# Two of the four weight sums of each seven-product group: made by adding transfers on GpSimd's queue in place of VectorE and GpSimd additions

## What is computed

```
first block :  x = x + relu(h @ ffn_w1)^2 @ ffn_w2           (8192 rows of ffn_w2)
second block:  x = x + norm((silu(gate) * val) @ ffn_w_down)  (5632 rows of ffn_w_down)
```

## Time and profile before

| | us |
|---|---|
| median of three runs | 2196.92 |
| the profiled execution's own time | 2197.45 |
| its span, first instruction to last | 2195.6 |
| TensorE busy in the span | 2180.6 |
| VectorE busy | 1566.8 |
| ScalarE busy | 1133.7 |
| GpSimd busy | 710.6 |

### The profile page before, as it was taken

The page is one execution under the profiler, slowest core; times in us unless marked ns, Lnnn a source line. Parts: engine busy times, 40 slices in busy tenths (PEclk is TensorE's granted clock), DMA queues, the critical chain, the costliest instruction groups (busy, mean ns, idle before and its releaser), DMA issues.

```text
span 2195.6 us, 34076 instructions
## 1 busy us (share of the span) xinstructions
PE 2180.6 (99%) x11511; PEld 1863.4 (85%) x11511; DVE 1566.8 (71%) x2187; ACT 1133.7 (52%) x1720; POOL 710.6 (32%) x625
## 2 busy tenths in 40 slices
PE   9999999999999999999999999999999999999998
PEld 8888988888888888888887887788888888888887
DVE  6877766558658757755868667568778777787775
ACT  6445555555445445444555455465555455554553
POOL 3202320361362263153000033005554355533531
PEclk9999999999999999999999999999999999999999
DMA  7665335556556556565555654545555655555554
GB/s 253 233 224 172 109 135 187 167 188 211 191 182 210 187 187 205 206 195 194 181 192 178 229 168 141 192 163 181 189 195 184 201 198 193 187 191 197 200 207 148
DMA packets 118084, 414.35 MB, mean 189 GB/s; under 512 B 12896, under 2 KB 18048, under 8 KB 117472
## 3 DMA queue, kind: packets, MB, share of 16 engines
q1 hardware_dynamic: 111600, 401.37, 54.4%
q10 hardware_dynamic: 6384, 11.70, 1.7%
HBM read 409.29 MB, written 2.15 MB: 187 GB/s over the span
## 4 chain that ended last, share of the span: by engine, by line
PE 91%; DVE 4%; POOL 2%; issue 2%; ACT 1%; DMA 0%; POOLq 0%; DVEq 0%; ACTq 0%
PE bank L607 31%; PE bank L615 16%; PE bank L941 6%; PE bank L943 6%; PE bank L942 6%; PE bank L664 3%; PE bank L666 3%; PE bank L665 3%; DVE wboth L1307 1%; POOL bias L2661 1%; PE bank L720 1%; PE bank L1269 1%; PE bank L1267 1%; PE bank L1268 1%; PE bank L721 1%
## 5 line engine op out<-in xcount | busy, mean ns | idle before, releaser
L1307 DVE TENSOR_TENSOR wboth<-raw,wboth 128x1024 fp32r<-128x1024 f32 (+1 forms) x756 | 954.2, 1267 | 470.5 <-ACT wboth L2157 462.2
L2157 ACT CAST wboth<-raw 128x1024 fp32r<-128x1024 f32 (+1 forms) x756 | 773.0, 1034 | 468.4 <-PE bank L943 123.9
L607 PE MATMUL bank<-A,wboth 128*128 128x512 f32 x2928 | 705.4, 392 | 0.5 <-DVE wboth L1307 0.3
L607 PEld LDWEIGHTS bank<-A,wboth 128*128 128x128 f32 x2928 | 536.8, 188 | 105.3 <-issue 1.3
L615 PEld LDWEIGHTS bank<-A,wboth 128*128 128x128 f32 x2928 | 376.7, 191 | 14.8
L615 PE MATMUL bank<-A,wboth 128*128 128x256 f32 x2928 | 384.0, 283 | 0.0
L941 PE MATMUL bank<-wboth,H 128*128 128x512 f32 x508 | 197.9, 389 | 1.2 <-DVE wboth L1307 1.2
L942 PE MATMUL bank<-wboth,H 128*128 128x512 f32 x508 | 197.7, 389 | 0.0
L943 PE MATMUL bank<-wboth,H 128*128 128x512 f32 x508 | 197.6, 389 | 0.0
L2661 POOL TENSOR_TENSOR PT<-z,rs 128x256 f32<-128x256 f32 x88 | 92.5, 1052 | 263.4 <-DVE z L1338 261.4
L2661 POOL TENSOR_TENSOR bias<-z,rs 128x256 f32<-128x256 f32 x64 | 104.7, 1635 | 197.8 <-DVE z L1338 109.4
(11 more groups left out here) (387 smaller groups left out, 3161.2 us busy)
## 6 DMA issues: line engine op xcount, KB each, us to landing
raw<-wstream SPq DMA_DIRECT2D x756, 512.0 KB, 3.3
bias<-bias_rows ACTq DMA_DIRECT2D x6, 512.0 KB, 5.4
x<-xrows ACTq DMA_DIRECT2D x1, 2048.0 KB, 10.6
bias<-grows ACTq DMA_DIRECT2D x2, 1024.0 KB, 6.5
out<-x SPq DMA_DIRECT2D x8, 256.0 KB, 2.1
x<-xT SPq DMA_DIRECT2D x7, 256.0 KB, 5.2
pA<-bias_rows ACTq DMA_DIRECT2D x2, 512.0 KB, 6.9
Sm<-grows ACTq DMA_DIRECT2D x1, 1024.0 KB, 6.9
```

What stands on the lines that cost most here:

```text
L607: last = nc.tensor.matmul(bank(j)[:, :], whi[:, s, cols(i)], moving(j, k), start=(k == 0), stop=(k == K - 1))
L1307: V.tensor_tensor(wlo[:, s, 0:w], raw[:, s, 0:w], whi[:, s, 0:w].bitcast(F32), ALU.subtract).then_inc(lo_ready, 1)
L2157: C.copy(whi[:, s, 0:w], raw[:, s, 0:w]).then_inc(hi_ready, 1)
```

## The change

Sums 0 and 1 of all 22 groups are now made by two transfers that GpSimd issues. The first, `t_load`, copies piece x once more from HBM into the sums' buffer, as (x0, x1). When it has landed, the second, `t_add`, reads the second halves of pieces x and y from HBM and adds them to what lies there, which gives (x0 + x1, x1 + y1). The additions of L1777, L1779, L2736 and L2738 are gone. `t_second`, `t_highs`, `t_lows` and the matmuls stay.

The load waits for the first of the two low-part instructions of the group before, where `t_first` waited for both. In FIRST the first group's load is issued ahead of `mix_low` and its adding transfer behind it; in SECOND both stand behind it. `t_second` and `t_highs` wait until the adding transfer has landed. `corners` of the first half now stands behind the third group's transfers in both kinds of stage; in FIRST it stood behind nothing but `mix_low`. Two semaphores change their places (`dn_half` and `t_sum`), with the same meaning.

```
             def down_pairs(c, fd, o):
-                summed = [0] if is_down2(c) else range(len(at.groups))
-                steps_of.update({at.at_x[g] - 4: lambda g=g: t_first(c, g) for g in summed})
                 steps_of.update({x - 3: lambda x=x, g=g: t_second(c, x, g) for x, g in at.x_at.items()})
                 ahead = {x + 2: lambda g=g: t_lows(c, g) for x, g in at.x_at.items()}
-                ahead.update({x: lambda g=g: dve.wait_ge(*t_sum.at(2 * group_of(c, g) + 2)) for x, g in at.x_at.items() if g not in summed})
...
             def t_second(c, i, g):
-                dve.wait_ge(*t_sum.at(2 * group_of(c, g) + (2 if is_down2(c) else 1)))
+                q = PB[fd] + i + 1
+                y = raw[:, q % SLOTS, :]
+                if g or not is_chunk(c, 0):
+                    dve.wait_ge(*t_lo.at(2 * group_of(c, g)))
+                dve.wait_ge(raw_landed[q % SLOTS], o * 256 + (q // SLOTS + 1) * 16)
+                dve.wait_ge(t_sum, 16 * group_of(c, g) + 16)
...
             def t_highs(c, g):
-                act.wait_ge(*t_sum.at(2 * group_of(c, g) + 2))
+                act.wait_ge(t_sum, 16 * group_of(c, g) + 16)
...
             def pair_sums(c):
-                for n in range(len(pairing(c).mixed)):
+                at = pairing(c)
+                if not is_down2(c):
+                    t_load(c, 0)
+                for n in range(len(at.mixed)):
                     mix_low(c, n)
-                for g in range(1, len(SECOND.groups)) if is_down2(c) else ():
-                    if g == SECOND.used(0) + 1:
+                if is_down2(c):
+                    t_load(c, 0)
+                t_add(c, 0)
+                for g in range(1, len(at.groups)):
+                    t_load(c, g)
+                    t_add(c, g)
+                    if g == at.used(0):
                         corners(c, 0)
-                    t_first(c, g)
-                for cp in (1,) if is_down2(c) else range(2):
-                    corners(c, cp)
+                corners(c, 1)
+
+            def t_load(c, g):
+                _, fd, o = stage_at(c)
+                i = o * 64 + (PB[fd] + pairing(c).at_x[g])
+                if g or not is_chunk(c, 0):
+                    pool.wait_ge(*t_lo.at(2 * group_of(c, g) - 1))
+                if is_down2(c) and g == 0:
+                    pool.wait_ge(*mix_ready.at(mix_count(c, len(SECOND.mixed))))
+                pool.dma_start(sums_at(c)[:, 0:2, :], wstream[ds(i, 1)].rearrange("a p (f n) -> p (a f) n", f=2)).then_inc(t_loaded, 16)
+
+            def t_add(c, g):
+                _, fd, o = stage_at(c)
+                i = o * 64 + (PB[fd] + pairing(c).at_x[g])
+                pool.wait_ge(t_loaded, 16 * group_of(c, g) + 16)
+                pool.dma_start(sums_at(c)[:, 0:2, :], wstream[ds(i, 2), :, WIDE:].rearrange("a p n -> p a n"), accum_op=ALU.add).then_inc(t_sum, 16)
```

More of the change, by code:

```diff
@@ L400, in program @@
         mix_sum, mix_hi, mix_ready = Again(acc_step, BLK), Again(pc_hi, 2 * KVG), Again(pad_zero, 1)
-        t_sum, t_more, t_hi = Again(c_taken, 5 * KVG), Again(cpad_zero, 1), Again(c_exp, KVG)
+        t_more, t_hi = Again(cpad_zero, 1), Again(c_exp, KVG)
+        t_loaded, t_sum = sem("t_loaded"), sem("t_sum")
         t_lo, t_used = Again(c_shift, KVG), Again(c_scores, KVG)
@@ L419, in program @@
         fin_rs, fin_out, out_done = (sem(n) for n in ("fin_rs", "fin_out", "out_done"))
-        dn_half = sem("dn_half")
+        dn_half = Again(c_taken, 5 * KVG)
         def main_bank(c, cp, j):
@@ L1283, in down2 @@
                             last = rows_of(k, 0)
-                        last.then_inc(dn_half, 1)
+                        last.then_inc(dn_half.sem, 1)
                         for k in range(FIN_SPLIT, n):
@@ L1765, in down_pairs, with t_second @@
                 rows_body(p, PB[fd], 32, 1, lambda f: None, steps_of, 0, ahead, at.x_at)
-            def t_first(c, g):
+            def t_second(c, i, g):
                 _, fd, o = stage_at(c)
-                i = pairing(c).at_x[g]
-                x, y = PB[fd] + i, PB[fd] + i + 1
+                q = PB[fd] + i + 1
+                y = raw[:, q % SLOTS, :]
                 if g or not is_chunk(c, 0):
                     dve.wait_ge(*t_lo.at(2 * group_of(c, g)))
[L1774 to L1783, removed]
-                dve.wait_ge(*t_sum.at(2 * group_of(c, g) + (2 if is_down2(c) else 1)))
+                dve.wait_ge(raw_landed[q % SLOTS], o * 256 + (q // SLOTS + 1) * 16)
+                dve.wait_ge(t_sum, 16 * group_of(c, g) + 16)
                 V.tensor_tensor(sums_at(c)[:, 2, :], sums_at(c)[:, 0, :], y[:, WIDE:], ALU.add).then_inc(t_more.sem, 1)
@@ L2128, in _ @@
                 if t == 0:
-                    dve.wait_ge(dn_half, 1)
+                    dve.wait_ge(*dn_half.at(1))
                 else:
```

## The result

The changed kernel takes 2323.22 us (median of 4 runs, 2320.90 to 2323.47); the kernel before, run beside it on the same chip, takes 2196.74 us (median of 4). The ratio is 1.0573, 95% interval [1.0561, 1.0586]: 126.5 us slower. The prediction said 2233 and a range of 2200 to 2270, so the sign was right and the size was wrong by a factor of 3.5.

A forecast was written before the change was run, and what follows sets the result against it. TensorE, busy 2180.6 of 2195.6 us, was taken as the bound, with lateness of the sums the question. Stalls by group summed to 35.9 us, on the profiled 2197.45 giving 2233.4, stated as 2233; range 2200 to 2270.

The forecast's parts named there:

- Lateness and not load: Whole kernel: what counts is whether sums arrive in time for TensorE; the change can win 1.2 us at most.
- T + 2.46: Each group: piece x + 1's low part is ready 2.46 us after the adding transfer has landed.
- T + 3.6: Each group: the sums' first low parts are made 3.6 us after the adding transfer lands; then the next load may start.
- The cover of 0.44 us: FIRST's first group: time left for the adding transfer behind `mix_low`; 2.65 and 2.77 us in the other two FIRST stages.
- The limit of 10.2: FIRST's fourth groups: 3.6 us spare, so no stall while load plus adding transfer take up to 10.2 us.
- the unknown price: Durations of GpSimd's transfers, not in the trace: load bounded by 3.3 and 5.4 us, adding transfer by 3.3 and 6.9.
- L = 9.2: Each group: load plus adding transfer, 4.0 and 5.2 us; four pieces behind another group, TensorE stalls by what exceeds 6.6.
- a = 8.1: Each group: the adding transfer's time, which the forecast put at 5.2 us.
- Within cover: Rival, at the wait ahead of `t_second`: transfers land within their cover, not slower; 2200.3 us, chance 0.18.
- The transfer queue as the bound: Rival, crowded group stretches: 10.9 us of transfers against TensorE's 10.2; 81 us of stalls, 2279 us, chance 0.22.
- stalls between groups: Sign in the profile after that would show the transfer queue to be the bound; no size given.
- VectorE holds off the making of descriptors: Rival, GpSimd's issues: each waits for a 1.2 us low part; 70 us, 2267 us, counted within the queue rival's 0.22.

The follow-up runs named there:

- experiment 10: Second buffer and early transfers in the three FIRST stages alone, SECOND as in the kernel before; 2198.02 us, ratio 1.0008.
- experiment 2: Changed kernel with the adding transfer left out, the load alone lets the sums go on (sums wrong); 2196.67 us, ratio 0.9997.
- experiment 9: Changed kernel with second buffer and early transfers, but SECOND's second group by GpSimd's two additions; 2200.61 us, ratio 1.0023.
- experiment 1: Changed kernel with the second transfer copying in place of adding (sums wrong); 2288.66 us, ratio 1.0417, two runs.
- experiment 7: Changed kernel with a second buffer, transfers of FIRST's first two groups and SECOND's first issued early, `corners` moved; 2204.89 us, ratio 1.0044.
- experiments 6: Changed kernel with a buffer of their own for sums 0 and 1 of even groups; 2245.79 us, ratio 1.0223.
- experiment 8: Kernel before plus one unused 8.67 us VectorE instruction ahead of `t_second` in each stage's first group, no transfers; 2241.06 us, ratio 1.0207.
- experiment 4: No transfers; GpSimd makes sums 0 and 1 of all 22 groups by additions; 2207.83 us, ratio 1.0049.

## Why the prediction was wrong

**What held.** Lateness and not load was the question, and that nothing could be won: no variant is faster than before. The waits are where they were foretold. T + 2.46 for the low part of x + 1 came out as 509.10 - 506.45 = 2.65 us, and T + 3.6 for the release of the next load as 510.24 - 506.45 = 3.8. The cover of 0.44 us in FIRST's first group: 8.08 - 0.44 = 7.64, and the stall was 7.64. To the last digit that is luck: the same working gives 5.2 and 5.3 us for the other two, which stalled by 5.98 and 6.20. Group 3 of each stage never stalled. The limit of 10.2 for FIRST's fourth groups was right too: with L of 12.9, 13.7 and 14.4 us there they do stall, by 2.91, 3.60 and 4.30, which makes 17 stalls of the forecast's 14. The DMA share of a FIRST stage without stalls is 0.76 in experiment 10, the number forecast.

**The step that failed first: the unknown price.** "L = 9.2" was 12.8 to 14.4 us in the twelve groups that follow another by four pieces, 13.3 on average (from the end of the first low part behind which the load waits to the landing of the adding transfer). Of its two parts the load was put at 4.0 and took 4.5 in the median, inside its bounds. The adding transfer was put at 5.2, with bounds of 3.3 and 6.9, and took 8.1, outside them. In the chain above the other 1.3 us are two gaps on GpSimd, 0.69 us from the release to the load's issue and 0.64 from its landing to the next issue; in SECOND the first gap is 0.28. I had taken landing to issue as nothing. Two things were wrong in the bound: it took transfers issued by other engines' hardware queues as the dearest, where this one spends 1.19 us in its issue alone, and it priced adding by its bytes, where the trace shows twice the packets.

With L = 13.3 and a = 8.1 the prediction's own terms give this (us; FIRST's first groups by 8.1 less 0.44 and 1.2, less 2.65, less 2.77; all others by their limits as stated there):

| groups | forecast at 9.2 | own terms at 13.3 | measured |
|---|---|---|---|
| first of FIRST, three | 8.6 | 17.2 | 18.6 |
| first of SECOND, two | 4.7 | 12.9 | 11.8 |
| second, five | 13.0 | 33.5 | 20.6 |
| fourth of FIRST, three | 0 | 9.3 | 10.8 |
| fourth of SECOND, two | 4.4 | 12.6 | 13.1 |
| fifth of SECOND, two | 5.2 | 13.4 | 8.1 |
| sum | 35.9 | 98.9 | 83.0 |

"Measured" are the 17 stalls of TensorE's timeline, less the old 1.2 us. By the prediction's own terms the mis-sized L is 98.9 - 35.9 = 63 us of error.

**The step that was missing: what a stall does to the matmuls behind it.** The sum counted matmuls at 0.227 us throughout, though a stall of several microseconds was part of the forecast. Behind 16 of the 17 the granted clock fell to 0.50 for 3 to 6 us, and of the 39.6 us of busy time some 36 are the slow pace there. It also explains the two rows of the table that are too high: in the seven groups right behind a stalled one, the slow matmuls lengthen the time that TensorE needs to get there (from 509.15 to 522.19 are 13.04 us, where I had 10.2), and so shorten the next stall by as much. In all seven that is about 18.4 us, and 98.9 - 18.4 = 80.5 is near the measured 83.0. What the longer busy time costs in the end is then 39.6 - 18.4, some 21 us: where the next wait ends by a transfer's landing, slow matmuls ahead of it are free. Together 99 + 21 = 120 of the span's 123.6 us; the last 3 to 4 us I have not placed.

**The rivals.**
- *Within cover*: refuted for the pair. For the load alone it is true (experiment 2).
- *The transfer queue as the bound*: its size, 81 us of stalls and L = 12.3, came nearest by accident of the numbers. As the bound of the kernel after it fails. Its own sign was stalls between groups, and all 17 stand at a group's piece x + 1; ScalarE waits for weight pieces there for 24.5 us, where it was 22.9 before. And in experiment 10 FIRST's stages carry load and adding transfer at a share of 0.76, and TensorE does not wait. What is true in it is that transfers lengthen each other's latency: the adding one lands in 5.5 us at best and 11.0 at worst, and in experiment 9, without the long waits for them, the weight pieces come late as well. How its 8.1 us divide between the two reads, the write and waiting behind weight pieces stays open; the runs bound only the addition's own part, 1.4 us in landing by experiment 1.
- *VectorE holds off the making of descriptors*: not seen. The issues of the kernel after take 585 to 743 ns and 1178 to 1204 ns. The adding one at 516.12 takes 1.20 us while VectorE stands still (514.2 to 523.9), and one of 1.19 us stands beside VectorE's low parts of 1666.59 to 1669.65 in experiment 7 (the row of GpSimd at 1666.85 above). Loads of about 1.03 us in experiments 6, 7, 9 and 10 are those issued some 0.75 us behind the start of an adding transfer's issue. With this the rule of the Trainium skill ("SBUF — State Buffer", "Who interferes with whom"), by which I called that rival void, agrees with the trace.
- The Trainium skill's price of a GpSimd-issued transfer ("DMA: Bandwidth & Descriptors", anatomy), an estimate of 3.2 us here, was under both rows, 4.5 and 8.1 us. The rule of the Trainium skill that an add runs at half the copy rate because of two source reads ("Collectives: The Full Stack", bandwidth ceiling) points the right way: 272 packets against 144, and about 2.4 times the engines' time over the whole kernel.

The range failed because both ends of L came from transfers of another kind, and because the stall was priced as idle time alone.

## What to carry to other kernels

Price a chained pair of transfers by its latency, from release to landing with both issues (here 13.3 us for two times 0.5 MB), and compare it with the cover at each place; a price nobody has measured deserves an upper bound well over the dearest row of another kind. If a buffer is shared from one use to the next, that latency is paid at every use, and a second buffer (77 us here) is worth more than a faster transfer. And price a long stall on TensorE (2.9 to 9.8 us here) as its length plus some 2.4 us of slow matmuls behind it (1.5 to 2.9 us behind 16 of the change's 17 stalls, nothing behind one), unless the next wait ends by something that does not depend on TensorE.

## What the runs showed that I had not expected

- The issue of an adding transfer takes 1.19 us on GpSimd, against 0.59 for the load and 0.71 for a copy with the adding one's shape.
- The adding transfer has about twice the packets of a copy of the same bytes (272 against 144) and takes about 2.4 times the transfer engines' time.
- Five stalls of 7 us on average cost 12.0 us more in slow matmuls (experiment 8), with TensorE at the 1.2 GHz level behind each; nine stalls of 2.0 us and less (experiment 4) cost 3.4 us. The length of the stall does not decide alone: the clock stayed at its full level behind one of 2.91 us and one of 2.02 us, and fell behind one of 1.88 us.
- With early transfers in 20 or 22 groups the weight pieces themselves come later: ScalarE waits 72.4 us for them in experiment 9 and 64.0 in experiment 7, against 22.9 before.
